# One decoder layer on one core: all four embedding gate blocks ahead of the expert loop, three expert weight buffers from the first pair

## What is computed

```
eidx, gw = route(x2, w_router, router_bias)          # 6 of 64 experts a token
ffn = swiglu(x2, w_s_gate, w_s_up, w_s_down)         # shared expert
      + routed_experts(x2, eidx, gw, w_e_gate, w_e_up, w_e_down)
ple = sigmoid(h @ w_ple_gate) * (p @ w_ple_proj)     # 1024 columns: 4 blocks of 256
h   = layer_norm(ALPHA * h + ffn + ple, ln2_g, ln2_b)
```

## Time and profile before

| | us |
|---|---|
| median of 3 runs (lowest, highest) | 1336.51 (1336.17, 1338.48) |
| the profiled execution, its own time | 1337.28 |
| span in its trace, first to last instruction | 1335.4 |
| PE, DVE, ACT, POOL busy | 1235.3, 495.5, 305.6, 129.7 |
| mean granted clock of PE | 0.975 |

### The profile page before, as it was taken

How to read it: one execution, slowest core, us unless ns; L and a number is a source line. 1 busy time by engine, 2 the same in 40 slices (tenths; PEclk the granted TensorE clock), 3 DMA queues, 4 the chain that set the end, 5 groups by cost and what they waited for, 6 DMA issues and landing times.

```text
span 1335.4 us, 23441 instructions
## 1 busy us (share of the span) xinstructions
PE 1235.3 (93%) x8867; PEld 999.6 (75%) x8868; DVE 495.5 (37%) x1089; ACT 305.6 (23%) x558; POOL 129.7 (10%) x200
## 2 busy tenths in 40 slices
PE   6999999999999999999889899989998799999846
PEld 6988879999999999998767667656665466666512
DVE  3456573423343333577862222111111111112127
ACT  3254453312222222133101111111111111111111
POOL 0200000000000000013101111111211111211100
PEclk8999999999999999999999999999999999999958
DMA  9222122231322133432357988999999999999775
GB/s 264 69 63 64 40 57 64 63 95 64 95 87 75 64 111 110 138 137 94 126 210 266 415 336 329 419 421 420 421 419 412 414 413 410 415 409 412 301 264 244
DMA packets 99475, 308.15 MB, mean 231 GB/s; under 512 B 11370, under 2 KB 62402, under 8 KB 73092
## 3 DMA queue, kind: packets, MB, share of 16 engines
q1 hardware_dynamic: 85844, 275.20, 53.9%
q0 software_dynamic: 12480, 28.60, 5.6%
q10 hardware_dynamic: 1088, 3.47, 0.8%
HBM read 295.95 MB, written 26.94 MB: 242 GB/s over the span
## 4 chain that ended last, share of the span: by engine, by line
PE 50%; DMA 39%; DVE 6%; DVEq 1%; issue 1%; ACT 1%; SPq 1%; POOLq 0%; ACTq 0%; POOL 0%
DMA w_exp<-in_w_e_down_dram 34%; PE proj L986 32%; PE proj L1154 4%; PE att L1286 3%; DMA part<-expert_rows 3%; PE att L1163 2%; PE proj L1359 2%; PE att L1079 1%; DMA pg_raw<-in_w_ple_gate_dram 1%; PE att L1041 1%; PE att L1342 1%; PE att L1154 1%; PE att L1092 1%; DMA xg<-x_rows,gidx_col 1%; DMA ident<-in_const_dram 0%
## 5 line engine op out<-in xcount | busy, mean ns | idle before, releaser
L1342 PE MATMUL att<-w_exp,xt 128*64 128x256 f32 x2560 | 289.3, 383 | 25.5 <-issue 13.1
L1342 PEld LDWEIGHTS att<-w_exp,xt 128*64 128x64 f32 x2560 | 220.7, 138 | 102.6 <-issue 48.4
L986 PE MATMUL proj<-h_hi,w_hi 128*128 128x288 f32 x800 | 179.6, 306 | 4.7 <-DVE h_lo L1394 4.7
L986 PE MATMUL proj<-h_hi,w_lo 128*128 128x288 f32 x800 | 171.9, 297 | 0.0
L986 PE MATMUL proj<-h_lo,w_hi 128*128 128x288 f32 x800 | 171.9, 297 | 0.0
L1359 PE MATMUL proj<-w_exp,ht_e 128*64 128x512 f32 x640 | 147.7, 602 | 10.8 <-DMA w_exp<-in_w_e_down_dram 6.0
L986 PEld LDWEIGHTS proj<-h_hi,w_hi 128*128 128x128 f32 x800 | 128.4, 190 | 21.1 <-issue 15.2
L986 PEld LDWEIGHTS proj<-h_lo,w_hi 128*128 128x128 f32 x800 | 129.9, 190 | 0.0
L986 PEld LDWEIGHTS proj<-h_hi,w_lo 128*128 128x128 f32 x800 | 129.6, 190 | 0.0
L444 DVE TENSOR_TENSOR w_lo<-w_raw,w_hi 128x2048 fp32r<-128x2048 f32 x33 | 75.6, 2291 | 95.9 <-ACT w_hi L434 89.5
L1359 PEld LDWEIGHTS proj<-w_exp,ht_e 128*64 128x64 f32 x640 | 50.8, 138 | 80.1 <-issue 77.9
(11 more groups left out here) (343 smaller groups left out, 1724.4 us busy)
## 6 DMA issues: line engine op xcount, KB each, us to landing
w_exp<-in_w_e_gate_dram SPq DMA_DIRECT2D x64, 1024.0 KB
w_exp<-in_w_e_up_dram SPq DMA_DIRECT2D x64, 1024.0 KB
w_exp<-in_w_e_down_dram SPq DMA_DIRECT2D x64, 1024.0 KB
w_raw<-in_w_in_dram SPq DMA_DIRECT2D x21, 1024.0 KB
part<-expert_rows SPq DMA_DIRECT2D x4, 3072.0 KB, 28.7
w_raw<-in_w_in_dram SPq DMA_DIRECT2D x8, 512.0 KB
w_raw<-in_w_attn_out_dram SPq DMA_DIRECT2D x8, 512.0 KB
w_raw<-in_w_conv_out_dram SPq DMA_DIRECT2D x4, 1024.0 KB
```

The lines of the kernel that those rows point to most:

```text
L986: last = nc.tensor.matmul(proj[:, 2 * i + a, 0:HALF], lhs, x[:, c, a * HALF:(a + 1) * HALF], start=(c == 0 and n == 0), stop=(c == KC - 1 ...
L1342: last = nc.tensor.matmul(att[e * SLOT:(e + 1) * SLOT, m, 0:FF], xt[:, c, e * SLOT:(e + 1) * SLOT], weights[e][:, c, :], start=(c == 0), s ...
```

## The change

All 20 gate units run before pair 0. PE alternates: unit 4 after table 0, then one unit after every two tables (units 5 to 8), units 9 to 14, the shared down products, turn(0), units 15 to 19. Every low part of a gate block and every product is POOL's. SP loads blocks 2 and 3 after units 4 and 9, pair 1's parts after routed, `ppo_added` and `sd_ready`, pair 2 (third buffer) after unit 19 and `res_done`. `hot` and its sum are bf16, the sum by three additions; ppo[0], hs_f and hs_hi move. `hs_lo` is made after `routed`. Cut:

```diff
-BUF_OF = (0, 1, 0, 1, 0, 1, 0, 2)
-RING = (1, 0, 2)
-GATE_SLOT = (1, 0, 0, 0)
+RING = (0, 1, 2)
+GATE_SLOT = (1, 0, 1, 0)
+N_BLK = D // GW
...
-        ppo = [at(f"ppo{i}", [P, NT, 512], F32, o) for i, o in enumerate((o_w1 + 32768, o_w2 + 36864))]
+        ppo = [at(f"ppo{i}", [P, NT, 512], F32, o) for i, o in enumerate((o_w1 + 28672, o_w2 + 36864))]
-        hs_f = at("hs_f", [P, 2, T], F32, o_w1 + 43008)
-        hs_lo = at("hs_lo", [P, 2, T], F32R, o_w1 + 43008)
-        hs_hi = at("hs_hi", [P, 2, T], F32R, o_x + 16384)
+        hs_f = at("hs_f", [P, 2, T], F32, o_w1 + 43520)
+        hs_lo = at("hs_lo", [P, 2, T], F32R, o_w1 + 43520)
+        hs_hi = at("hs_hi", [P, 2, T], F32R, o_w1 + 38912)
...
-        hot = rsm("hot", [P, NTK, NE], F32)
-        assert next_routing[0] <= o_w1 + 32768
+        hot = rsm("hot", [P, NTK, NE], BF16)
+        hot_a = at("hot_a", [P, NT, TOPK // 2, NE], BF16, o_w1 + 4096)
+        hot_b = at("hot_b", [P, NT, NE], BF16, o_w1 + 4096 + 2 * NT * TOPK // 2 * NE)
+        assert next_routing[0] <= o_w1 + 28672
...
         def gate_bank(u):
-            return proj[:, 2 + u % 2, 0:GW] if u < NT else att[:, 2 + u % 2, 0:GW]
+            return proj[:, 2 + u % 2, 0:GW]
...
-            load_gate(0)
-            sp.wait_ge(pp_mm, 2 * NT)
-            load_gate(1)
-            sp.wait_ge(su_ready, 2)
-            for n in range(4):
-                load_part(0, 0, n)
-            sp.wait_ge(routed, 1)
-            for n in range(4):
-                part_landed(1, n)
-                load_part(1, 1, n)
-            sp.wait_ge(sd_ready, 2 * NT)
-            for n in range(4, 6):
-                load_part(0, 0, n)
+            def load_parts(p, i, parts):
+                for n in parts:
+                    if p:
+                        part_landed(p, n)
+                    load_part(p, i, n)
...
-            def landed_and_load(p, parts):
-                for n in parts:
-                    part_landed(p, n)
-                    load_part(p, BUF_OF[p], n)
-            done = sp.value_load(cum_pass[0:1, 0:1], min_val=1, max_val=MAXPASS - 1)
-            sp.wait_ge(gu_ready, done)
-            past(nc.sync, 4)
-            landed_and_load(2, range(4))
+            load_gate(0)
+            sp.wait_ge(pp_mm, 2 * NT)
+            load_gate(1)
+            sp.wait_ge(su_ready, 2)
+            load_parts(0, 0, range(4))
+            sp.wait_ge(u_ready, NT)
+            load_gate(2)
+            sp.wait_ge(u_ready, 2 * NT)
+            load_gate(3)
+            sp.wait_ge(routed, 1)
+            load_parts(1, 1, range(3))
             sp.wait_ge(ppo_added, 1)
-            landed_and_load(1, range(4, 6))
-            landed_and_load(2, range(4, 6))
-            sp.wait_ge(u_ready, 2 * NT)
-            load_gate(2)
-            for p in range(3, 7):
-                next_pair(p, BUF_OF[p], p - 2)
-                if p == 4:
-                    sp.wait_ge(u_ready, 3 * NT)
-                    load_gate(3)
-            sp.wait_ge(u_ready, 4 * NT)
+            load_parts(1, 1, range(3, 4))
+            sp.wait_ge(sd_ready, 2 * NT)
+            load_parts(0, 0, range(4, 6))
+            load_parts(1, 1, range(4, 6))
+            sp.wait_ge(u_ready, N_BLK * NT)
+            load_parts(2, 2, range(4))
             sp.wait_ge(res_done, 1)
-            for n in range(6):
-                part_landed(7, n)
-                load_part(7, BUF_OF[7], n)
-            with sp.Fori(0, (NPE - 8) // 3) as it:
+            load_parts(2, 2, range(4, 6))
+            for p in range(3, 5):
+                next_pair(p, RING[p % 3], p - 3)
+            with sp.Fori(0, (NPE - 5) // 3) as it:
                 for i in range(3):
-                    next_pair(it * 3 + (8 + i), RING[i], it * 3 + (5 + i))
+                    next_pair(it * 3 + (5 + i), RING[(5 + i) % 3], it * 3 + (2 + i))
...
-            pool.wait_ge(pw_hi, 1)
-            i = GATE_SLOT[0]
-            nc.gpsimd.tensor_tensor(pg_lo[i][:, :], pg_raw[i][:, :], pg_hi[i][:, :].bitcast(F32),
-                                    ALU.subtract).then_inc(pw_lo_pool, 1)
+            def gate_lo(j):
+                i = GATE_SLOT[j]
+                pool.wait_ge(pw_hi, j + 1)
+                nc.gpsimd.tensor_tensor(pg_lo[i][:, :], pg_raw[i][:, :], pg_hi[i][:, :].bitcast(F32),
+                                        ALU.subtract).then_inc(pw_lo_pool, 1)
+            gate_lo(0)
             pool.wait_ge(pp_mm, 2 * NT)
             nc.gpsimd.memset(xg[:, :, :], 0.0).then_inc(x_zero, 1)
-            for u in range(NT):
+            gate_lo(1)
+            for u in range(2 * NT):
                 ple_product(u)
+                if u == NT + 1:
+                    gate_lo(2)
             pool.wait_ge(routed, 1)
...
             gather(0, 0, 1)
+            for u in range(2 * NT, N_BLK * NT):
+                ple_product(u)
+                if u == 2 * NT + 1:
+                    gate_lo(3)
             pool.wait_ge(xtr, 1)
             gather(1, 1, 2)
...
                 i = GATE_SLOT[j]
-                act.wait_ge(pw_in[i], 16 * max(j, 1))
+                act.wait_ge(pw_in[i], 16 * (j // 2 + 1))
...
-            for u in range(NT):
+            for u in range(N_BLK * NT):
                 gate_sigmoid(u)
-            act.wait_ge(hs_ready, 2)
-            nc.scalar.activation(hs_hi[:, :, :], hs_f[:, :, :], ACT.Copy).then_inc(hs_hd, 1)
-            xt_half(0)
+                if u == NT - 2:
+                    act.wait_ge(hs_ready, 2)
+                    nc.scalar.activation(hs_hi[:, :, :], hs_f[:, :, :], ACT.Copy).then_inc(hs_hd, 1)
+                if u in (NT + 1, 2 * NT + 1):
+                    gate_hi(u // NT + 1)
+                if u == 3 * NT - 1:
+                    xt_half(0)
...
-            for p in range(5):
+            for p in range(2):
                 passes(p)
-                if p in (1, 3):
-                    gate_hi(2 + p // 3)
-                if p in (0, 2, 4):
-                    for u in range((1 + p // 2) * NT, (2 + p // 2) * NT):
-                        gate_sigmoid(u)
             for i, g in enumerate((ln2_g, ln2_b)):
                 act.dma_start(g2b2[:, i, :], g[0].partition_broadcast(P)).then_inc(ld_ln2, 16)
-            with act.Fori(0, NPE - 5) as it:
-                passes(it + 5)
+            with act.Fori(0, NPE - 2) as it:
+                passes(it + 2)
...
                 if t == 0:
-                    if j == 0:
-                        pe.wait_ge(pw_lo_pool, 1)
-                    else:
-                        pe.wait_ge(pw_lo_dve, j)
+                    pe.wait_ge(pw_lo_pool, j + 1)
...
             for u in range(NT - 1):
                 gate_unit(u)
             pe.wait_ge(rank_read, 1)
-            for m in range(NTK // TPAIR):
+            table_products(0)
+            for m in range(1, NTK // TPAIR):
+                if m % 2:
+                    gate_unit(NT - 1 + m // 2)
                 table_products(m)
-                if m == 1:
-                    gate_unit(NT - 1)
+            for u in range(2 * NT - 1, 3 * NT):
+                gate_unit(u)
...
                 wide_products(*sd_w, t, c, hs_hi, hs_lo, sd_bank(n)[0:w, :]).then_inc(sd_ready, 1)
             pe.wait_ge(routed, 1)
             turn(0)
+            for u in range(3 * NT, N_BLK * NT):
+                gate_unit(u)
             pe.wait_ge(sd_read, 2 * NT)
-            pe.wait_ge(u_sig, NT)
+            pe.wait_ge(u_sig, N_BLK * NT)
...
-            for p in range(8):
-                pair(p, BUF_OF[p])
-                if p in (0, 2, 4):
-                    for u in range((1 + p // 2) * NT, (2 + p // 2) * NT):
-                        gate_unit(u)
-                    pe.wait_ge(u_sig, (2 + p // 2) * NT)
-            with pe.Fori(0, (NPE - 8) // 3) as it:
+            for p in range(2):
+                pair(p, RING[p])
+            with pe.Fori(0, (NPE - 2) // 3) as it:
                 for i in range(3):
-                    pair(it * 3 + (8 + i), RING[i])
+                    pair(it * 3 + (2 + i), RING[(2 + i) % 3])
...
-            def gate_lo(j):
-                i = GATE_SLOT[j]
-                dve.wait_ge(pw_hi, j + 1)
-                nc.vector.tensor_tensor(pg_lo[i][:, :], pg_raw[i][:, :], pg_hi[i][:, :].bitcast(F32),
-                                        ALU.subtract).then_inc(pw_lo_dve, 1)
             dve.wait_ge(sw_hi_done, 3)
             nc.vector.tensor_tensor(sw_lo[2][:, :], sw_raw[2][:, :], sw_hi[2][:, :].bitcast(F32),
                                     ALU.subtract).then_inc(sd_lo_done, 1)
-            gate_lo(1)
...
             dve.drain()
-            with nc.allow_low_precision(reason="each sum is 0 or 1, exact in bfloat16"):
-                nc.vector.reduce_sum(sel[:, :, :], hot[:, :, :].rearrange("p (t j) e -> p t e j", t=NT), AX.X).then_inc(sel_ready, 1)
+            hot5 = hot[:, :, :].rearrange("p (t j) e -> p t j e", t=NT)
```

(58 more changed lines are left out.)

## The result

| | before | after |
|---|---|---|
| median, us (runs; lowest, highest) | 1336.72 (12; 1334.94, 1339.66) | 1340.80 (12; 1339.08, 1343.61) |
| the profiled execution, its own time | 1337.28 | 1339.26 |
| span in its trace | 1335.4 | 1337.4 |

The ratio is 1.0032, 95% interval 1.0021 to 1.0043: slower by 4.1 us, 0.3%. The forecast was +0.8 with a range of 1330 to 1343; the time is inside the range, but outside the band of 0.2% in which I put the result: it lies in "slower", to which I had given 0.27.

The account below looks back on a forecast made before the run. Engine order bounds the kernel until the weight stream becomes unbroken, then the stream does. Unit 19's end, 660.1 + 72.5 + 3.5 = 736.1 against a break-even 735, plus 532 of stream gave +1 us: 1337.5 median, range 1330 to 1343.

Parts of the forecast that it names:

- (1): Ahead of the routing: POOL's subtraction for gate block 1's low part holds DVE, so `biased` starts 3.45 us late.
- (2): One-hot sum on DVE: three bf16 additions take 2.2 us instead of the reduction's 3.62, a gain of 1.4.
- (4): Alternating tables and gate units: POOL's low part of block 2 holds DVE's eighth table, and PE stands about 3.5 us.
- (3): PE's work from first table product to end of unit 19: tables, units, down products, turn and clock loss, 72.5 us.
- G: The end of gate unit 19, from which the weight stream runs unbroken; forecast at 736.1 us.
- G + 532: End of the weight stream: 30 pairs need 532 us after unit 19, 445.0 for 25 plus 87 for five more.
- the foundation: The stream's end is its unbroken start plus a fixed time; wrong if the last landing misses by over 3 us.
- A: Rival at the routing and the tables: POOL doesn't hold DVE, so the time is 1330 us; chance 0.32 with its halves.
- B: Rival at unit 14: block 3's copy on ACT holds the sigmoids, 1343 us; chance 0.27 together with a second clock dip.
- C: Rival in the stream: the third buffer does nothing early and three buffers could leave gaps; no chance of its own.

Follow-up runs that it names:

- e1: Changed kernel with gate block 1's low part made by DVE again instead of POOL: 1339.84 us, ratio 1.0021 to before.
- e2: Changed kernel with the low parts of gate blocks 1 and 2 on DVE, block 2's behind routed: 1332.56 us, ratio 0.9974 to before.
- e5: Changed kernel with the products of units 15 to 19 made twice, no byte more: 1354.46 us, ratio 1.0148 to before.
- e8: Changed kernel with block 1's low part on DVE and block 2's on POOL two units later, behind DVE's tables: 1335.09 us, ratio 0.9993 to before.
- e4: Changed kernel with pair 0 ahead of units 15 to 19, pair 2 in buffer 0, low parts 1 and 2 on DVE: 1330.88 us, ratio 0.9959 to before.
- e4b: The kernel of e4 measured again, beside e9: 1330.04 us, ratio 0.9947 to before.
- e6: Changed kernel with two buffers in turn for pairs 0 to 6, the third only from pair 7: 1345.27 us, ratio 1.0068 to before.
- e9: The kernel of e4 with the shared down products moved ahead of units 10 to 14: 1332.29 us, ratio 0.9966 to before.
- e3: Changed kernel with pair 0 put ahead of units 15 to 19 and pair 2 in buffer 0: 1336.62 us, ratio 0.9999 to before.
- e7: Kernel before the change with only the bf16 one-hot and its sum by three additions: 1336.26 us, ratio 0.9997 to before.

## Why the prediction was off

**Step by step, counted from R** (the prediction's own times less 606.63):

| step of the prediction | said | measured in after |
|---|---|---|
| (1) `biased` late by POOL's product | +3.45 | +3.07 (14.24 after R; 11.17) |
| (2) gain of the bf16 sum | 1.4 (2.2 by the Trainium skill's rate) | 2.2 (16.03 to 13.84 from `biased` to sel) |
| first table product later by | +2.05 | +0.87 (52.31; 51.44) |
| (4) PE stands beside block 2's low part | 3.5 | 3.78 (2.58 + 1.20) |
| (3) and (4) first table product to G | 76.0 | 76.7 |
| G from R | 129.5 | 129.04 |
| 30 pairs from the first issue to the last landing | 532 | 535.34 |

Steps 1 and 2, the timeline of DVE in after:

```profile
...
615.23 3.72 DVE L1674 CAST tri_b<-cc 128x128 bf16<-128x128 f32 x1 [8.00 <-PE att L1231]
618.87 0.22 DVE L1675 CAST ones_b<-cc 128x128 bf16<-128x128 f32 x1
...
619.32 0.49 DVE L1679 TENSOR_TENSOR biased<-scores,rbias 128x320 f32<-128x320 f32 x1
...
631.69 0.66 DVE L1725 TENSOR_TENSOR hot_a<-hot 128x960 bf16<-128x960 bf16 x1
632.43 0.33 DVE L1727 TENSOR_TENSOR hot_b<-hot_a 128x320 bf16<-128x320 bf16 x1
632.83 0.33 DVE L1729 TENSOR_TENSOR sel<-hot_b,hot_a 128x320 bf16<-128x320 bf16 x1
...
```

The timeline of POOL in after:

```profile
...
614.27 4.58 POOL L664 TENSOR_TENSOR pg_lo<-pg_raw,pg_hi 128x2048 fp32r<-128x2048 f32 x1
...
674.63 4.63 POOL L664 TENSOR_TENSOR pg_lo<-pg_raw,pg_hi 128x2048 fp32r<-128x2048 f32 x1 [1.06 <-ACT pg_hi L894]
...
```

The cast `tri_b`, 128 elements a partition, takes 3.72 and ends 0.1 after POOL's subtraction; the next cast takes 0.22. So the hold takes in the casts. The Trainium skill (GPSIMD Engine Reference, Key points) names contention with DVE instructions in a two-port mode or with two SBUF inputs. The trace agrees in that this cast, with one SBUF input, was held; in which mode it ran, no row shows. At the tables the last product of the eighth table, 0.44 alone, takes 4.63 from 674.93 (in the chain above), and POOL's row is 674.63 to 679.26. Full stops, not half speed.

Step 2: 0.66 for 960 elements, 0.33 for 320. An f32 addition of 320 took 0.48. By the rows the bf16 additions cost 0.52 ns an element ((0.66 - 0.33) / 640), f32 ones 1.05 ((2.29 - 0.48) / 1728). The Trainium skill (VectorE: DVE Perf Modes, The perf-mode tier table) gives bf16 tensor_tensor twice the f32 rate; the trace agrees. My extrapolation from an f32 row was 0.8 too dear.

Step 4, the timeline of PE in after:

```profile
...
657.39 2.01 PE L1269 MATMUL proj<-tab_b,tab_a 128*128 128x180 f32 x6 [3.87 <-DVE tab_b L1823]
...
679.62 1.18 PE L1269 MATMUL proj<-tab_b,tab_a 128*128 128x180 f32 x6 [2.58 <-DVE tab_b L1823]
682.00 2.17 PE L1269 MATMUL proj<-tab_b,tab_a 128*128 128x180 f32 x6 [1.20 <-DVE tab_b L1823]
...
```

The stand of 2.58 and the 1.20 behind it are the predicted 3.5. They cost a second dip (the six matmuls at 682.00 take 2.17 and the next six 0.92, the unit between them 3.22 instead of 2.83), which I had only among the rivals. It is some 1.6 inside the 76.7. That 76.0 and 76.7 lie so close is in part luck: the units (2.83 to 2.85 instead of 2.89), the down products (13.67 instead of 13.9) and the turn (0.89 instead of 1) came about 1 cheaper and hid most of it. G itself came out right because this and the first table, 1.2 earlier than said, nearly cancel.

**The term that failed is G + 532.** "Five pairs come 2 us under 89, and I take 87": they cost 535.34 - 444.97 = 90.4, 18.1 a pair. The constant is 534.9 to 536.0 in the five traces with three buffers and 30 pairs (after, e1, e2, e5, e8), so this is no matter of one run, though two traces of one kernel, e4 and e4b, differ by 2.5 in it.

The bytes were about right. From S to L before moves 181.5 MB and after 217.4 MB: 35.9 MB for five pairs, of which 31.5 are weights and the rest six scatters and seven gathers. That is 86 us at 416 GB/s. What is left is the rate, and the windows above show where: up to the landing of pair 10 both kernels stream at 416 GB/s (76.06 us before, 165.14 after). Behind it before has 406 and after 402. The work there is the same 21 pairs with 28 gathers and 28 scatters; after takes 1.3 us longer for it, although it has 1.1 MB less of it left when pair 10 has landed. 1% of 370 us is 3.7 us, about the miss.

From 829 to 1236 the same shows as 416 GB/s before and 412 after (in this window before also runs about one pass more, 126 DVE instructions against 122, so the bytes are not quite the same). e1, e2, e4, e5, e6, e8 and e9 have 412 or 413 there, e3 and e4b 411, e7, which has the gates where before has them, 416. So the rate goes with the gates' place, not with the buffer ring (e6 has the old one), nor with the bf16 sum. The evidence is thin in two points: e4 and e4b, one kernel, differ by 2 GB/s themselves, and the higher rate is seen in two traces only. Why the loop streams 1% slower stays open; I found nothing in the rows that tells, and made no run for it.

Put together, from R: G came 0.4 earlier than said, the stream took 3.3 more, 2.9 in sum; 1337.5 + 2.9 = 1340.4, measured 1340.8. I wrote that the foundation would fail beyond 3 us, "that is if a pair costs other than 17.7", and it missed by 3.3. e5 shows that the form of the law is right, and its constant was the error: the term took over before's mean rate for the loop.

**The rivals.** A (POOL doesn't hold DVE) is ruled out by the two stops and by e2 and e8. B (block 3's copy holds the sigmoids) did not happen: block 3 was asked for at 691.1 and ACT's copy began at 697.1, so the weights had landed within 6.0 us, and B counts from 9.5 on. Instructions on the tile pg_raw in after, ns min/median/max:

```profile
...
L894 ACT ACTIVATE pg_hi<-pg_raw x4: 1904/1910/1920, 606.8 to 697.1; 128x2048 fp32r<-128x2048 f32 x4
...
```

The second dip of the clock, which I had put into B's chance, did, but the other terms hid it in G. So the outcome on B's side came by another way than B's, by the rate of the stream. C gave nothing before G, as said, and no gap; but the third buffer is worth 4.5 us right after G (e6), because the first load there need not wait for pair 0. Without it the change would have cost 8.9 (e6 against before of its group).

The answer to what the change does: it puts 43 us of units in front of the stream that ran beside it, moves the stream's start by 86 us for five pairs that need 90, and loses on the way some 6 us to DVE standing beside POOL (e8 against after). Once that is mended the idea is level with before (e8) or 0.3% faster (e2), and 0.4 to 0.5% faster with pair 0 ahead of block 3 as well (e4, e4b).

## What to carry to other kernels

When a kernel has a stretch that its DMA stream bounds, cost every edit by the moment at which the stream becomes unbroken, and double one piece of work there once to see that the law holds. Price the stream's length by rate and bytes apart: a 1% slower rate over 370 us is as much as the whole effect. Put POOL's long elementwise instructions where DVE is idle or off the chain: the same subtraction two units later was worth 5 us.

## What was not expected

- Time won on the chain ahead of a stretch of short PE work did not all arrive: e1 and e7 won 2.8 and 1.8 us at the first table and had 1.7 and 0.6 of it left at the end of the stage, with a second dip of the clock between (mean of the 45 us 0.89, where after has 0.92 and before 0.96). In e2 and e8, whose PE does not stand between the tables, it is 0.96. Whether the dip is the cause is not shown: e3, with after's order, has 0.89 too.
- The hold by POOL takes in a small cast: 3.72 us for 128 elements a partition that take 0.2 alone.
- The same loop streams at 416 GB/s (829 to 1236) when 15 of the gate units lie between its first pairs and at 411 to 413 when all stand in front; the difference begins only behind pair 10, long after the last unit, and its cause is open.
